# Probabilities of two attentions turned by VectorE and by transfers instead of by TensorE, in three of four rounds each

## Chip, cores and metric

The kernel runs on one core of one Trainium2 chip. The metric is the device time of one execution in microseconds (us), the median of several. A core has five engines with a queue each: TensorE (PE; its weight loads are shown as PEld), VectorE (DVE), ScalarE (ACT), GpSimd (POOL) and SyncE (SP). SP and POOL also issue the transfers (DMA).

## What is computed

Two blocks of a network over 512 tokens of width 1024, in float32. Cut to the parts that the change touches:

```python
# first block: 8 heads of 64, in 4 pairs
q = rms_norm(q, g_q) * 64 ** -0.5; k = rms_norm(k, g_k)
# three dilated causal branches, merged: the kernel computes them as one attention,
# softmax(q k^T + log(number of branches that see the key)) v
y_attn = dilated_mixture(q, k, v)
mix = concat([rms_norm(gb * short_conv(gc * u)), rms_norm(y_attn)])
x = x + mix @ w_out
# second block: 8 heads share one key and one value of 64
p = softmax(where(key in top 128 of the indexer, q k^T * 64 ** -0.5, -inf))
yb = (p @ v) * silu(zb)
```

The modulation of the second block, `silu(c) @ w_mod`, is also summed up during the first attention, on VectorE, from rows that POOL loads.

## The kernel before

**Products.** Almost every product is a `project`: a weight block of 1024 x 128 is loaded (SP, `load`, 512 KB), split into a high part (ACT, `split_hi`) and a low part (DVE, `split_lo`), and multiplied in 24 passes of 512 columns into a PSUM bank (lines 591 to 593). There are two weight buffers for each of raw, high and low part. The high part of block n+2 is made once TensorE has used block n, the low part after it; TensorE waits for `lo_done`. Everything is ordered by semaphores, and each engine works its queue in the order that is written out by hand in its own program.

**First attention, `mix(i, last)`, four rounds, a pair of heads each.** TensorE: three projections (u, gc, gb of the convolution), the transposition of the values into `vtok`, the scores of both heads (`split_scores`: q and k were split into `q1`, `k1`, `k1L` by ACT and DVE, so that two fast passes do for a product), the projections q, k, v of the next pair, then `attend`, then `head_sums` (sums of squares of the next q and k). `attend` does, per head, ten transpositions of 128x128 blocks of the probabilities `L` into four PSUM banks (line 568), which ACT copies out to `pT` (`p_evac`, eight copies), and then the products with the values (line 657). Causality leaves 10 of 16 blocks: a head has 1280 columns of `L`, at `CB`.

DVE in `mix`: `qk_norm`, the low parts of q and k, splits and the convolution, `score_max` (adds the mask, takes the maximum, writes `L`), `mod_rows` (6 rows of the modulation a round, each 128x1024, from `mraw`), `normalise` (times the reciprocal sum, in place). ACT: `head_rsqrt`, the high parts of q and k, `softmax` (exponentials), `p_evac`, and at the round's end the copy and the square of the attended values (`yo`, `sqa`, `mixH`). POOL: `mod_loads`, the six transfers of `mraw` a round, each as soon as its buffer is free.

**Second attention, `att(i, last)`, four rounds.** TensorE: the gate's product (`glu`, 24 passes, the scores of key blocks 2 and 3 in its middle), the projection of the next q, `attend`, and the scores of blocks 0 and 1 of the next pair. Scores here are plain float32 products of 64 rows (`scores`, line 625). DVE: `normalise`, the gate (`sza`), `head_max` with the gating of the attended values (`gate_out`) in its middle. In the last round the projection's place is taken by products of the next stage (`ab_terms`).

```python
def attend(a, v, vcol):
    for hh in range(2):
        pe.wait_ge(pn, a * 2 + (hh + 1))
        for kb in range(TB):
            pe.wait_ge(t_free, a * 8 + (4 * hh + kb + 1))
            transposes(TBANK[kb], [L[:, hh, CB[b] + P * kb:CB[b] + P * kb + P] for b in range(kb, TB)]).then_inc(tr_mm, 1)
    wait(pe, o_free, a + 1)      # the bank of the attended values has been read
    ...                          # products with the values, into OB
```

Of the kernel before, what the change touches and what calls it, by code (L numbers as in the profile page):

```python
# [16 lines left out]
F32 = mybir.dt.float32  # L17
# [59 lines left out]
OFF = [0, 512, 896, 1152, 1280]  # L77

# [49 lines left out]
def program(nc, io):  # L128
# [7 lines left out]
    with ExitStack() as ctx:  # L136
# [34 lines left out]
        mx, nmx, rs, rinv = (at(n, [P, 8]) for n in ("mx", "nmx", "rs", "rinv"))  # L171
# [44 lines left out]
        ybL = at("ybL", [P, KH, S], F32R, B0 + 31744)  # L216
# [13 lines left out]
        q1 = [at(f"q1{e}", [P, S], F32R, B0 + 26624 + 2048 * e) for e in range(2)]  # L230
        k1 = [at(f"k1{e}", [P, S], F32R, B0 + 30720 + 2048 * e) for e in range(2)]
        k1L = [at(f"k1L{e}", [P, S], F32R, B0 + 34816 + 2048 * e) for e in range(2)]
# [41 lines left out]
        q_hi, q_lo, qx_hi, kx_hi = (sem(n) for n in ("q_hi", "q_lo", "qx_hi", "kx_hi"))  # L274
        vtr, vt_done, ych = sem("vtr"), sem("vt_done"), sem("ych")
        sc_ready, sc_free, nm, ex, pn = (sem(n) for n in ("sc_ready", "sc_free", "nm", "ex", "pn"))
# [53 lines left out]
        def freed(eng, s):  # L330

            eng.wait_ge(gfree[s.par], s.gf + 1)

# [90 lines left out]
        def _(pool):  # L424
# [15 lines left out]
            def mod_loads(i):  # L440
# [110 lines left out]

            pool.wait_ge(yb_done, KH)
# [9 lines left out]
        def _(pe):  # L562
# [71 lines left out]
            def split_scores(a):  # L634

                for hh in range(2):
                    for b in range(TB):
                        pe.wait_ge(sc_free, a * 8 + (4 * hh + b + 1))
                        split_score(SB[b], b, q1[hh], k1[hh], k1L[hh]).then_inc(sc_ready, 1)

# [3 lines left out]
            def attend(a, v, vcol):  # L644

                for hh in range(2):
                    pe.wait_ge(pn, a * 2 + (hh + 1))
                    for kb in range(TB):
                        pe.wait_ge(t_free, a * 8 + (4 * hh + kb + 1))
                        transposes(TBANK[kb], [L[:, hh, CB[b] + P * kb:CB[b] + P * kb + P] for b in range(kb, TB)]  # L650
                                   ).then_inc(tr_mm, 1)
                wait(pe, o_free, a + 1)
                for kb in range(TB):
                    pe.wait_ge(t_free, a * 8 + (kb + 9))
                    for hh in range(2):
                        r = slice(HD * hh, HD * hh + HD)
                        ins = mm(OB[r, P * kb:S], v[:, kb, vcol(hh)], pT[:, hh, OFF[kb]:OFF[kb + 1]],  # L657
                                 start=(kb == 0), stop=(kb == TB - 1), skip_group_check=True)
                        if kb == TB - 1:
                            ins.then_inc(pv, 1)  # L660
# [50 lines left out]
            def mix(i, last):  # L711
                for j in range(3):
                    project(Slot(3, j, 6, i))
                freed(pe, Slot(2, 0, 6, i))
                transposes(PB[3], [vT[:, blkc(b)] for b in range(TB)]).then_inc(vtr, 1)
                pe.wait_ge(ss_rd, i * 2 + 2)
                pe.wait_ge(xt_done, KD)
                pe.wait_ge(q_lo, i + 1)
                split_scores(i)
# [52 lines left out]
            with pe.Fori(0, NPAIR - 1) as i:  # L772
                mix(i, False)
            mix(NPAIR - 1, True)
# [198 lines left out]
            scores(NPAIR, qn, kn)  # L973
            project(Slot(N_AT))
            pe.wait_ge(yg_rdy, KH)
            pe.wait_ge(ya_done, KH)

# [92 lines left out]
        def _(act):  # L1070
# [104 lines left out]
            def mix(i, last):  # L1175
# [13 lines left out]
                if not (isinstance(i, int) and i == 0):  # L1189
                    wait(act, ych, i + 1)  # L1190
# [1120 lines left out]
```

## Time and profile before

| | |
|---|---|
| median of 3 runs | 1002.49 us (1002.38 to 1002.98) |
| the profiled execution | 1004.4 us, span 1001.6 us |
| PE busy | 983.9 us, 98% of the span |
| DVE, ACT, POOL busy | 684.2, 439.1, 157.7 us |
| transposition of the probabilities on PE (L568, `L`) | 160 instructions, 20.3 us |
| granted clock | 0.999 |

The span is the time from the first to the last instruction of the profiled execution. A row of the timeline gives the start, the duration, the engine and line, what is written from what, and in brackets the idle time before it and what ended it. PE instructions overlap: each lasts longer than the distance to the next start, so distances of starts are what counts. A float32 product is recorded twice, a transposition once.

### The profile page before, as it was taken

To read this page: it belongs to the slowest core of one execution; us is meant where nothing else is said; L and a number is where in the kernel's file an instruction comes from. 1 tells how busy PE (TensorE), PEld (TensorE's weight loads), DVE (VectorE), ACT (ScalarE), POOL (GpSimd) and SP (SyncE) were. 2 spreads that over 40 slices of the span, in tenths; PEclk is the share of its full clock that TensorE was granted. 3 is DMA by queue.
4 is the path that set the end of the run, shared out by engine and by line. 5 is a ranking of instruction groups with operands and counts; after the bars stand their busy time and mean duration, and the time that the engine had idled before them with its cause. 6 is when DMAs were issued, how large, how long until landed. Compare 5 with 4: busy or idle time off the path is not lost. (4 is left out here: it accounts for less than half of the span.)

```text
span 1001.6 us, 14462 instructions
## 1 busy us (share of the span) xinstructions
PE 983.9 (98%) x4732; PEld 798.4 (80%) x4732; DVE 684.2 (68%) x1221; ACT 439.1 (44%) x729; POOL 157.7 (16%) x274
## 2 busy tenths in 40 slices
PE   6999999999999999999999999999999999999997
PEld 6887787777888888888888877888888887677886
DVE  7787786797667667555426668498978764665656
ACT  5656666644323233233221236945542325563343
POOL 3000100200000000964000001835750000000000
PEclk9999999999999999999999999999999999999999
DMA  7244624352533323244223223322233332123332
GB/s 229 85 144 130 204 76 139 77 155 73 178 100 90 105 85 104 88 143 149 88 102 102 86 75 109 102 85 65 63 105 96 92 105 63 43 64 86 106 93 84
DMA packets 144305, 104.31 MB, mean 104 GB/s; under 512 B 4717, under 2 KB 136045, under 8 KB 144269
## 3 DMA queue, kind: packets, MB, share of 16 engines
q1 hardware_dynamic: 138768, 85.83, 29.1%
q0 software_dynamic: 5264, 17.97, 6.0%
q8 instruction: 19, 0.31, 0.1%
q14 instruction: 18, 0.14, 0.0%
q10 hardware_dynamic: 236, 0.06, 0.0%
HBM read 99.65 MB, written 4.20 MB: 104 GB/s over the span
## 5 line engine op out<-in xcount | busy, mean ns | idle before, releaser
L591 PE MATMUL bank<-hH,wH 128*128 128x512 f32 x840 | 328.7, 391 | 0.1
L593 PE MATMUL bank<-hH,wL 128*128 128x512 f32 x840 | 327.0, 389 | 0.0
L592 PE MATMUL bank<-hL,wH 128*128 128x512 f32 x840 | 326.9, 389 | 0.0
L1506 DVE TENSOR_TENSOR wL<-raw,wH 128x1024 fp32r<-128x1024 f32 x155 | 196.1, 1266 | 129.2 <-ACT wH L1074 128.2
L1074 ACT ACTIVATE wH<-raw 128x1024 fp32r<-128x1024 f32 x155 | 164.2, 1059 | 264.4 <-PE bank L593 136.1
L591 PEld LDWEIGHTS bank<-hH,wH 128*128 128x128 f32 x840 | 157.7, 188 | 36.9 <-issue 2.9
L593 PEld LDWEIGHTS bank<-hH,wL 128*128 128x128 f32 x840 | 157.7, 188 | 32.9
L592 PEld LDWEIGHTS bank<-hL,wH 128*128 128x128 f32 x840 | 157.8, 188 | 32.1
L835 PE MATMUL bank<-aH,wH 128*128 (+1 forms) x160 | 62.2, 389 | 0.0
L836 PE MATMUL bank<-aL,wH 128*128 (+1 forms) x160 | 62.2, 389 | 0.0
L837 PE MATMUL bank<-aH,wL 128*128 (+1 forms) x160 | 62.2, 389 | 0.0
L1817 DVE TENSOR_TENSOR ut<-bank,r 128x512 f32<-128x512 f32 x22 | 15.2, 691 | 50.4 <-PE bank L593 50.4
L443 POOL DMA_DIRECT2D mraw<-in_w_mod_dram x24 | 12.7, 530 | 199.4 <-DVE macc L1685 199.1
L1165 ACT ACTIVATE L<-L,nmx 128x128 f32<-128x128 f32 (+1 forms) x64 | 35.1, 550 | 12.1 <-DVE nmx L1667 11.3
L1685 DVE SCALAR_TENSOR_TENSOR macc<-mraw,csil,macc 128x1024 f32<-128x1024 f32 x24 | 30.3, 1281 | 8.9 <-DMA mraw<-in_w_mod_dram 8.9
L835 PEld LDWEIGHTS bank<-aH,wH 128*128 128x128 f32 x160 | 30.0, 188 | 6.3
L837 PEld LDWEIGHTS bank<-aH,wL 128*128 128x128 f32 x160 | 30.0, 188 | 6.2
L836 PEld LDWEIGHTS bank<-aL,wH 128*128 128x128 f32 x160 | 30.0, 188 | 6.2
L1074 ACT ACTIVATE aH<-a 128x512 f32 (+1 forms) x22 | 13.9, 632 | 45.6 <-DVE a L1821 45.6
L498 POOL COPY yaF<-yg 32x128 f32<-32x128 f32 x64 | 32.8, 512 | 2.9
L1823 DVE TENSOR_TENSOR aL<-a,aH 128x512 fp32r<-128x512 f32 (+1 forms) x22 | 17.0, 771 | 18.3 <-ACT aH L1074 18.3
L553 POOL DMA_DIRECT2D gate_row<-mod x1 | 0.8, 764 | 166.6 <-DVE ybL L2181 166.6
(478 smaller groups left out, 1548.5 us busy)
## 6 DMA issues: line engine op xcount, KB each, us to landing
raw<-in_w_in_dram SPq DMA_DIRECT2D x61, 512.0 KB, 3.6
mraw<-in_w_mod_dram POOLq DMA_DIRECT2D x24, 512.0 KB, 4.6
raw<-in_w_gate_dram SPq DMA_DIRECT2D x22, 512.0 KB, 3.7
raw<-in_w_up_dram SPq DMA_DIRECT2D x22, 512.0 KB, 3.7
raw<-in_w_down_dram SPq DMA_DIRECT2D x22, 512.0 KB, 3.3
raw<-in_w_out_dram SPq DMA_DIRECT2D x16, 512.0 KB, 3.5
x_tok<-in_x_dram SPq DMA_DIRECT2D x4, 512.0 KB, 5.6
rotations<-eb POOLq DMA_DIRECT2D x4, 512.0 KB, 5.0
```

Of the source, the lines that this page charges most:

```text
L498: ins = g.tensor_copy(dst(a, b), src(a, b))
L591: mm(o, a, hH[:, k, :], start=(k == 0), stop=False)
L592: mm(o, a, hL[:, k, :], start=False, stop=False)
L593: ins = mm(o, b, hH[:, k, :], start=False, stop=(k == KD - 1))
L835: mm(PB[d][:], blk(wH[s], d), rh, start=a, stop=False, skip_group_check=True)
L836: mm(PB[d][:], blk(wH[s], d), rl, start=False, stop=False, skip_group_check=True)
L837: ins = mm(PB[d][:], blk(wL[s], d), rh, start=False, stop=False, skip_group_check=True)
L1074: return A(o, i_, ACT.Copy, scale=scale)
L1165: ins = A(l, l, ACT.Exp, bias=nmx[:, c:c + 1], accum_out=rs[:, c:c + 1])
L1506: TT(wL[s.par][:], raw[s.par][:], wH[s.par][:].bitcast(F32), SU).then_inc(lo_done, 1)
L1685: STT(o, mraw[m % 2][:], col(csil, i * 2 + m // 3), o, MU, AD).then_inc(m_used, 1)
L1823: TT(dyn(aL, i), a32[:], dyn(aH, i).bitcast(F32), SU).then_inc(a_done, 1)
```

## The change

In three of four rounds of each attention the probabilities are turned without TensorE and weighed a round later.

- DVE transposes `L` in pieces of 32x32 (`turn`, four instructions a head) into `turned` (second attention: `turned2`). POOL then issues four transfers a round (`turned_moves`), each from 32 partitions of `turned` to all 128 of `pTd`, 1.31 MB in all. They leave the keys of a block in another order (key 32j+c on partition 4c+j), and so the values are put in that order as well: in the copy to `vT`, in the copy of `kvraw` (now two copies), and in products with a permuted identity for the last round of each attention.
- TensorE weighs pair i-1 in round i (`weigh(..., pieces=True)`): in `mix` after the projection of gc, in `att` after the projection of q. `attend` is left for the last rounds, which also weigh the pair before.
- POOL holds the loads of modulation rows 2 to 5 back until the round's moves have landed; DVE does rows 2 to 5 in the next round.
- The scores of the first attention are plain float32 products, as in the second; the split copies of q and k go.
- The negated maximum is taken in one step, and `softmax` runs block by block over both heads.
- In the second attention ACT scales the second head (three rounds), one reciprocal serves both heads, and `gate_out` and `gated_low` come a round later.

```diff
+        turned = at("turned", [P, TB, 2 * NB, 32], F32, B0 + 26624)
+        pTd = at("pTd", [P, TB, 2 * NB, 32], F32, B0 + 10240)
...
+        def places(hh, qb):
+
+            return slice(1 + qb, 1 + qb + 5 * qb + 1, 5) if hh == 0 else slice(5 * qb, 6 * qb + 1)
+
+        def place_of(hh, kb):
+
+            return slice(5 * kb + 1 + kb, 5 * kb + 1 + TB) if hh == 0 else slice(6 * kb, 5 * (TB - 1) + kb + 1, 5)
...
+            def turned_moves(a, src):
+
+                pool.wait_ge(turn_rdy, 2 * TB * (a + 1))
+                settled(pool)
+                for q in range(TB):
+                    pool.dma_start(pTd[:, q].rearrange("p b c -> p (b c)"),
+                                   src[32 * q:32 * q + 32].rearrange("p j b c -> p j (b c)")).then_inc(turn_in, 16)
...
+                    if m == 2 and between is not None:
+                        between()
...
+            def moves_then_wait(i):
+                pool.wait_ge(o_free, i + 1)
+                turned_moves(i, turned)
+                pool.wait_ge(turn_in, 16 * TB * (i + 1))
+                settled(pool)
             with pool.Fori(0, NPAIR - 1) as i:
-                mod_loads(i)
+                mod_loads(i, lambda: moves_then_wait(i))
...
+            for i in range(NPAIR - 1):
+                pool.wait_ge(pv, 2 * (NPAIR + i))
+                turned_moves(NPAIR - 1 + i, turned2)
...
+            def weigh(a, v, vcol, pieces=False):
+
+                wait(pe, o_free, a + 1)
+                for kb in range(TB):
+                    for hh in range(2):
+                        r = slice(HD * hh, HD * hh + HD)
+                        p = (pTd[:, :, place_of(hh, kb), :].rearrange("p i b c -> p b i c") if pieces
+                             else pT[:, hh, OFF[kb]:OFF[kb + 1]])
+                        ins = mm(OB[r, P * kb:S], v[:, kb, vcol(hh)], p,
+                                 start=(kb == 0), stop=(kb == TB - 1), skip_group_check=True)
...
+            def mix(i, first, last):
+                project(Slot(3, 0, 6, i))
+                project(Slot(3, 1, 6, i))
+                if not first:
+                    pe.wait_ge(turn_in, 16 * TB * i)
+                    weigh(i - 1, vtok, pair_cols, True)
+                project(Slot(3, 2, 6, i))
...
+                if last:
+                    for b in range(TB):
+                        for j in range(TB):
+                            ins = mm(PB[3][32 * j:32 * j + 32, blkc(b)], vT[:, P * b + j:P * b + P:TB], ident,
+                                     start=True, stop=True, skip_group_check=True)
+                    ins.then_inc(vtr, 1)
+                else:
+                    transposes(PB[3], [vT[:, blkc(b)] for b in range(TB)]).then_inc(vtr, 1)
...
-                split_scores(i)
+                pe.wait_ge(qn_rdy, i * 2 + 2)
+                scores(i, qn, kn)
...
-                attend(i, vtok, lambda hh: slice(HD * hh, HD * hh + HD))
-                if not last:
+                if last:
+                    attend(i, 0, vtok, pair_cols)
+                else:
                     head_sums(i + 1, Slot(7, 0, 6, i))
...
             scores(NPAIR, qn, kn)
+            for j in range(TB):
+                ins = mm(PB[3][32 * j:32 * j + 32, 0:TB * HD], ident[:, j:P:TB], vt2[:].rearrange("p b n -> p (b n)"),
+                         start=True, stop=True, skip_group_check=True)
...
-                attend(i + NPAIR, vt2, lambda hh: slice(0, HD))
-                if not last:
+                if begun:
+                    pe.wait_ge(turn_in, 16 * TB * (i + (NPAIR - 1)))
+                    weigh(i + (NPAIR - 1), vt2, head_cols, True)
+                if last:
+                    attend(i + NPAIR, 1, vt2n, head_cols)
+                else:
                     freed(pe, Slot(N_AT + 1, 1, 2, i))
                     scores(i + (NPAIR + 1), qn, kn, range(2))
...
-                copy(vT[:], PB[s[2].par][:]).then_inc(gfree[s[2].par], 1)
+                copy(vT[:].rearrange("n (b p j) -> n b p j", b=TB, j=TB),
+                     PB[s[2].par][:].rearrange("n (b j p) -> n b p j", b=TB, j=TB)).then_inc(gfree[s[2].par], 1)
...
+                for u, (hh, b) in enumerate(order):
+                    act.wait_ge(sc_free, a * 8 + (u + 1 + 4))
+                    c = 4 * hh + b
+                    l = L[:, hh, CB[b]:CB[b + 1]]
+                    ins = A(l, l, ACT.Exp, bias=nmx[:, c:c + 1], scale=-1.0, accum_out=rs[:, c:c + 1])
...
-            copy(kvraw[:], PB[0][:]).then_inc(gfree[0], 1)
+            copy(kvraw[0:HD, :], PB[0][0:HD, :])
+            copy(kvraw[HD:P, :].rearrange("n (b p j) -> n b p j", b=TB, j=TB),
+                 PB[0][HD:P, :].rearrange("n (b j p) -> n b p j", b=TB, j=TB)).then_inc(gfree[0], 1)
...
+                if not last:
+                    act.wait_ge(rinv_rdy, i + 1)
+                    for b in range(TB):
+                        l = L[:, 1, CB[b]:CB[b + 1]]
+                        ins = A(l, l, ACT.Copy, scale=rinv[:, 4 + b:5 + b])
+                    ins.then_inc(pn_act, 1)
...
+                if last:
+                    p_evac(1)
                 freed(act, s)
                 copy(dyn(y2H, i), dyn(sza, i), 0.5).then_inc(y2h, 1)
...
+            def turn(hh, qb, to=turned):
+
+                v.transpose(to[:, :, places(hh, qb), :].rearrange("p j b c -> p b j c"),
+                            L[:, hh, CB[qb]:CB[qb + 1]].rearrange("p (b j c) -> p b j c", j=TB, c=32)
+                            ).then_inc(turn_rdy, 1)
...
+                    if turning is not None:
+                        if hh:
+                            turning()
+                        dve.wait_ge(pn, a * 2 + (hh + 1))
+                        for b in range(TB):
+                            turn(hh, b)
...
+                if not first:
+                    mod_rows(i - 1, range(2, 4))
                 split_lo(u.next())
...
+                if not first:
+                    mod_rows(i - 1, range(4, 6))
                 used(gb)
...
-                if not last:
-                    mod_rows(i, range(0, 2))
-                normalise(i)
+                if last:
+                    values_low(i - 1)
+                normalise(i, None if last else lambda: split_lo(Slot(3, 3, 6, i).next()))
...
+                    mod_rows(i, range(0, 2))
...
+                    dve.wait_ge(turn_in, 16 * TB * (i + (NPAIR - 1)))
+                    dve.wait_ge(pn, a * 2 + 1)
+                    for b in range(TB):
+                        turn(0, b, turned2)
+                    dve.wait_ge(pn_act, i + 1)
+                    for b in range(TB):
+                        turn(1, b, turned2)
...
                 if last:
-                    gate_out()
+                    gate_out(i - 1)
+                    gated_low(i - 1)
+                    gate_out(i)
+                    gated_low(i)
```

## Rows read from the trace of the kernel before

**Rows 1.** The page: busy time, share of the span, instructions
```profile
PE 983.9 (98%) x4732; PEld 798.4 (80%) x4732; DVE 684.2 (68%) x1221; ACT 439.1 (44%) x729; POOL 157.7 (16%) x274
```
**Rows 2.** Who TensorE waited for: total us, times, longest
```profile
PE bank L575 <- ACT thg L1414: 0.6, 1, 0.6
```
**Rows 3.** Timeline of PE, first attention, rounds 0 and 1
```profile
54.47 0.30 PE L631 MATMUL bank<-k,q 128*128 128x128 f32 x1
...
57.48 0.40 PE L591 MATMUL bank<-hH,wH 128*128 128x512 f32 x1
...
73.82 1.25 PE L568 MATMUL bank<-cst,L 128*128 128x128 f32 x10
...
76.56 2.37 PE L657 MATMUL bank<-pT,vtok 128*64 128x512 f32 x16
...
79.89 0.50 PE L591 MATMUL bank<-hH,wH 128*128 128x512 f32 x1
80.22 0.40 PE L592 MATMUL bank<-hL,wH 128*128 128x512 f32 x1
```
**Rows 4.** Timeline of PE, second attention, round 0 and its end
```profile
844.47 1.25 PE L568 MATMUL bank<-cst,L 128*128 128x128 f32 x10
...
847.30 2.38 PE L657 MATMUL bank<-pT,vt 128*64 128x512 f32 x16
849.61 0.93 PE L625 MATMUL bank<-kn,qn 64*128 64x128 f32 x8
```
**Rows 5.** Timeline of all engines, eight scores in a row before the second attention
```profile
825.06 3.02 PE L625 MATMUL bank<-kn,qn 64*128 64x128 f32 x16
```
**Rows 6.** Timeline of PE, products with 32 output rows
```profile
603.98 1.96 PE L876 MATMUL bank<-s5W,cTt 128*32 128x128 f32 x64
```
**Rows 7.** Timeline of all engines around the copy of `kvraw`
```profile
621.14 0.60 ACT L1074 ACTIVATE kvraw<-bank 128x512 f32<-128x512 f32 x1 [2.34 <-PE bank L921]
621.79 0.19 PEld L591 LDWEIGHTS bank<-hH,wxH 128*128 128x128 f32 x1 [0.47 <-ACT kvraw L1074]
```
**Rows 8.** Groups by line and form, ACT: busy us, mean ns
```profile
L1074 ACT ACTIVATE s5U<-xaP 32x128 f32<-32x128 f32 x32 | 13.6, 426 | 0.3
```
**Rows 9.** Groups by line and form, DVE
```profile
L1869 DVE STREAM_TRANSPOSE mtr<-macc 128x1024 f32<-128x1024 f32 x3 | 3.7, 1238 | 0.0
```
**Rows 10.** Timeline of DVE, first attention, round 0
```profile
61.42 2.48 DVE L1685 SCALAR_TENSOR_TENSOR macc<-mraw,csil,macc 128x1024 f32<-128x1024 f32 x2
63.81 0.17 DVE L1672 RECIPROCAL rinv<-rs 128x4 f32<-128x4 f32 x1
...
66.61 1.22 DVE L1506 TENSOR_TENSOR wL<-raw,wH 128x1024 fp32r<-128x1024 f32 x1
...
69.77 1.28 DVE L1685 SCALAR_TENSOR_TENSOR macc<-mraw,csil,macc 128x1024 f32<-128x1024 f32 x1 [0.75 <-DMA mraw<-in_w_mod_dram]
```
**Rows 11.** Timeline of POOL, first attention, round 0
```profile
63.34 0.53 POOL L443 DMA_DIRECT2D mraw<-in_w_mod_dram  x1 [47.03 <-DVE macc L1685]
```
**Rows 12.** Line 443, the loads of `mraw` (24 of 512 KB)
```profile
DMA to landing us min/median/max: 3.8/4.6/7.1
```
**Rows 13.** Windows: us, busy of PE, PEld, DVE, ACT, POOL, clock, DMA
```profile
79.89:122.12 42.23, 42.02 (x213) 33.22 (x209) 32.52 (x57) 26.56 (x54) 3.17 (x6) 1.00 0.52 151
849.61:868.50 18.89, 18.68 (x102) 13.35 (x101) 12.17 (x35) 11.41 (x30) 0.00 (x0) 1.00 0.20 57
```
**Rows 14.** Timeline of DVE, second attention, round 1 and the last
```profile
858.01 0.18 DVE L1672 RECIPROCAL rinv<-rs 128x4 f32<-128x4 f32 x1 [0.60 <-ACT L L1165]
...
904.80 0.69 DVE L2169 SCALAR_TENSOR_TENSOR y2L<-sza,y2H 128x512 fp32r<-128x512 f32 x1 [2.91 <-ACT y2H L1074]
```
**Rows 15.** Timeline of ACT, second attention, round 0 and the last
```profile
844.67 0.60 ACT L1074 ACTIVATE qn<-bank 128x512 f32<-128x512 f32 x1 [3.71 <-PE bank L593]
...
901.42 2.83 ACT L1074 ACTIVATE pT<-bank 128x512 f32<-128x512 f32 x8 [1.92 <-PE bank L568]
```
**Rows 16.** Timeline of PE, second attention, last round
```profile
903.57 2.37 PE L657 MATMUL bank<-pT,vt 128*64 128x512 f32 x16
```

More of the change, by code:

```diff
@@ L648, in attend @@
                     for kb in range(TB):
-                        pe.wait_ge(t_free, a * 8 + (4 * hh + kb + 1))
+                        pe.wait_ge(t_free, n * 8 + (4 * hh + kb + 1))
                         transposes(TBANK[kb], [L[:, hh, CB[b] + P * kb:CB[b] + P * kb + P] for b in range(kb, TB)]
                                    ).then_inc(tr_mm, 1)
[L652 to L660, printed above, removed]
+                pe.wait_ge(t_free, n * 8 + 12)
+                weigh(a, v, vcol)
             for s in (ix_ready, xf_tr):
@@ L1169, in p_evac, with values_out @@
+            by_head = [(hh, b) for hh in range(2) for b in range(TB)]
+            in_turn = [(hh, b) for b in range(TB) for hh in range(2)]
+            def p_evac(t):
                 for hh in range(2):
                     for kb in range(TB):
-                        act.wait_ge(tr_mm, a * 8 + (4 * hh + kb + 1))
+                        act.wait_ge(tr_mm, t * 8 + (4 * hh + kb + 1))
                         n = S - P * kb
                         copy(pT[:, hh, OFF[kb]:OFF[kb + 1]], TBANK[kb][:, 0:n]).then_inc(t_free, 1)
-            def mix(i, last):
+            def values_out(a):
+                act.wait_ge(pv, a * 2 + 2)
+                copy(yo[:], OB[:])
+                A(sqa[:], OB[:], ACT.Square)
+                A(dyn(mixH, a + KH), OB[:], ACT.Identity, scale=vec[:, bass.ds(a + V_GATT, 1)]).then_inc(o_free, 1)
@@ L1187, in mix @@
-                key_high(0)
                 used(u)
-                if not (isinstance(i, int) and i == 0):
+                if not first:
                     wait(act, ych, i + 1)
@@ L1427, in att @@
                     split_hi(t.next())
-                act.wait_ge(o_free, i + (NPAIR + 1) + 1)
-                copy(dyn(ybH, i), dyn(szb, i)).then_inc(ybh, 1)
-                if not last:
-                    softmax(i + (NPAIR + 1))
-            with act.Fori(0, NPAIR - 1) as i:
-                att(i, False)
-            att(NPAIR - 1, True)
+                if not first:
+                    act.wait_ge(o_free, i + (NPAIR + 1))
+                    copy(dyn(ybH, i - 1), dyn(szb, i - 1)).then_inc(ybh, 1)
+                if last:
+                    act.wait_ge(o_free, i + (NPAIR + 2))
+                    copy(dyn(ybH, i), dyn(szb, i)).then_inc(ybh, 1)
+                else:
+                    softmax(i + (NPAIR + 1), in_turn)
+            att(0, True, False)
+            with act.Fori(1, NPAIR - 1) as i:
+                att(i, False, False)
+            att(NPAIR - 1, False, True)
             with act.Fori(0, KD // 2) as i:
@@ L1711, in mix @@
                 mark(STT(cv[:], cuP[:, 0:S], col(vec, i + V_CONV), cv[:], MU, AD))
+                if not first:
+                    mod_rows(i - 1, range(4, 6))
                 used(gb)
```

204 lines of the change are left out of this document (94 added, 110 removed).

## The prediction

> **What bounds the kernel now.** I read the page first: TensorE is busy for 983.9 of 1001.6 us [rows 1], so only what leaves its queue, or opens a gap in it, moves the time. The list of what TensorE waited for is short; the one entry that the change touches is 0.6 us for ACT's tanh in the last round of the second attention [rows 2]. Then the timelines of TensorE around `attend`. In the first attention the transpositions of a round begin at 73.82 and the products with the values at 76.56 [rows 3]: 2.74 us, twice the 1.25 of ten transpositions and 0.24 of waiting for `p_evac`. In the second they run from 844.47 to 847.30: 2.83 us [rows 4]. The windows of a round say how much room the helpers have: DVE is busy for 32.5 of 42.2 us in a round of `mix`, for 12.2 of 18.9 us in a round of `att`, and the clock is at its full level (1.00, so 2.4 GHz) in both [rows 13]. So TensorE's share can be read off directly, and the doubt is whether DVE, ACT and the transfers stay hidden in rounds that get shorter.
>
> **What TensorE no longer does.** Twenty transpositions in each of six rounds. Three rounds at 2.74 and one at 2.83 [rows 3, 4]; the other two of `att` I take at 2.75, the same pattern. Together 16.5 us. The products with the values stay, 2.31 us a round (847.30 to 849.61 [rows 4]), only later. They now read `pTd` in runs of 32 columns with jumps between them. No row shows such a read by TensorE; below it is bounded by no extra cost (these products stream at float32's slow pace, so reading is hardly their limit), above by half as much again, 6 × 1.15 = 7 us. I take none.
>
> **Scores of the first attention.** Split, they take 57.48 − 54.47 = 3.01 us a round [rows 3]; as plain products, the same eight before the second attention are busy for 3.02 us with an overlap into what follows [rows 5], about 2.95 by starts. Four rounds: −0.2 us. ACT and DVE lose the split copies, over 4 us of DVE a round, which is what pays for the turning.
>
> **What TensorE gets or waits for.**
> - A change from float32 products to the split passes costs a slower first pass: 0.33 us from 79.89 to 80.22 [rows 3] where 0.23 is usual (16.34 us from 57.48 to 73.82 for 72 passes). Weighing in the middle of the projections adds one such change in three rounds: +0.3.
> - The permuted values of the last round: 16 products of 128 columns with 32 output rows. 64 records of that form (32 products) take 1.96 us [rows 6], so 0.98, for four transpositions of about 0.13 (10 in 1.25 [rows 3]), with their start 0.36: +0.6. The four of 256 columns before the second attention: +0.5 by the same row, 1.0 at most if the four column groups did not overlap.
> - `kvraw`: TensorE already waits for this copy (0.47 [rows 7]), and it becomes two. The first is as before but for half the partitions, the second adds 0.5 at the contiguous pace (0.60 less the overlap), and it reads PSUM at a distance of 32 elements. ACT's copies `s5U<-xaP` read at a distance of four and take 426 ns for 128 columns [rows 8], against some 310 for a contiguous 128 (0.60 for 512 less 384 columns at 0.83 ns, plus a little for SBUF): about twice as long per column. So +0.5 to +1.0; I take +0.8. The Trainium skill (SBUF — State Buffer, Door 1) says that SBUF lines are 16 bytes and PSUM's 8, and that every step to another line costs; the row agrees in direction, and the sum by the page would be the upper end. The same slow read in `vT`'s copy lies behind the v projection, with `p_evac` gone from its place (2.83 [rows 15]): hidden.
> - `att(0)`: `attend` stood between the projection of q and the next scores and hid ACT's copy of `qn` (844.67, 0.60 [rows 15]) out of the bank. In round 0 nothing is weighed, so the scores wait until about 845.4 where the projection ended at 844.47: +0.9. Later rounds have `weigh` there.
> - The last round of `att`. `weigh` of the last pair waits on `o_free`, now for `gate_out` of the pair before, whose place in DVE's queue is behind `y2L`; `y2L` waits for ACT's `y2H`, and that stands behind the eight copies of `p_evac` [rows 15]. In the trace `y2L` starts at 904.80 [rows 14]; `gate_out` behind it, 0.6 later and 0.69 long, ends at 906.1, and with 0.1 of signalling TensorE may weigh at 906.2 instead of 903.57 [rows 16]: +2.6. This is a new wait and the largest cost.
> - The tanh wait goes: the exponentials begin on the first blocks while the last maxima are still being taken, and end some 2 us earlier: −0.6 [rows 2].
>
> **Sum.** −16.5 − 0.2 + 0.3 + 0.6 + 0.5 + 0.8 + 0.9 + 2.6 − 0.6 = −11.6 us. The profiled execution took 1004.4 us with a span of 1001.6; the median of the runs is 1002.49, close to the span. I take the difference off the median: 990.9, say 991.
>
> **Does the rest stay hidden, first attention.** *Turning.* A 32x32 transposition of 128x1024 takes 1.24 us on DVE [rows 9], one column per 1.2 ns with its fixed part. Four of 128 to 512 columns are about 1.7 us a head by that pace (1280 columns and four starts); upper bound for the scattered writes, twice that. *The weights of v.* In the old order normalising begins at 63.81, after 2.48 us of modulation rows, and v's low part is made at 66.61 [rows 10]. Now those rows come later: two normalisations (1.4 each, half of 63.81 to 66.61) and the turning of head 0 (1.9 with its wait) end at about 66.0, the split at 67.2; v begins at 68.4 (57.48 + 10.9). Held, with 1.2 us in hand. *The moves.* Head 1 is turned by about 68.8. POOL then issues four transfers, 1.31 MB. No row shows SBUF to SBUF; the nearest is the pair of `mraw` loads issued from 63.34 on [rows 11], whose second lands at 69.77 [rows 10]: 1.05 MB in 6.4 us, so 8 us here. Bounds from the landing times: 3.8 to 7.1 us for 512 KB [rows 12]; four quarter-megabyte-and-more moves in series at the slow end are 4 × 0.625 × 7.1 = 18 us, at the quick end 6. *Behind them* on POOL stand the loads of modulation [rows 2] and 3. With 8 us the moves end at 76.8, the loads land at 81.4 and 82.6, and DVE, which now has these rows in its queue ahead of gb's split, is done with them at 83.9 and with the split at 85.1. The next round's u begins at 79.89 − 5.05 = 74.85, gb 13.2 later at 88.05. So 2.9 us in hand: moves of up to 11 us cost nothing, and each further microsecond costs one in each of three rounds. The Trainium skill speaks against these moves: by SBUF — State Buffer, Door 1, 32 partitions reach only 8 of the 16 ports, about 218 GB/s at best, and a transfer has some 2 us fixed. An estimate by that page is 1.31 MB / 218 GB/s + 2 = 8 us, no longer than the estimate from rows.
>
> **Second attention.** DVE's 12.2 us a round [rows 13] become 12.2 + 3.6 − 1.2 = 14.6, in a round of 18.9 − 2.75 = 16.1. The chain: exponentials done by about 858 instead of 860, one reciprocal (where 858.01 stands now [rows 14]), head 0 scaled (1.2), both turned (3.6), the gate (0.69 as `y2L` [rows 14]), the split (1.2 [rows 10]), the gate's last step (0.69): free bank at about 865.5. The next gate product starts less than 1 us after 868.50 − 2.75 = 865.75, so about 866.6: held by 1 us. ACT's scaling of head 1 (four copies, about 1.5) runs beside DVE's 2.9 us on head 0. Moves end well ahead of `weigh`.
>
> **Rivals.**
> 1. *DVE becomes the bound.* Were the scattered turning to take twice 1.7 us a head, v's weights would come 0.5 late in three rounds, the moves' margin would be short by 0.5, and `att` would wait about 2.4 us in three rounds: +10, about 1001. For it: both margins are near 1 us. Against: the output still comes in runs of 32, and 1.24 us for 1024 is the plain pace. Smaller versions (+1 to +4) fit between. Together 17%.
> 2. *The moves are slow but not fatal.* 12 to 14 us each: +3 to +10, 994 to 1001. For it: four transfers from 32 partitions each beside weight loads. 12%.
> 3. *Slower than before.* At 18 us, the slow end of [rows 12], gb's weights come 7 us late in three rounds: +21, about 1012. It decides from 15 us on, where 3 × 3.9 eats the gain. 7%.
> 4. *Weighing in pieces is slow*: up to +7, 998. 6%.
> 5. *The turning does not take place off the path at all*, so that no change shows: nothing in the queues speaks for it; 1%.
>
> **Numbers.** My forecast holds with 57%, at 991, with 989.5 to 993 as its own range (the lower end with cheap copies of `kvraw`, the upper with `kvraw` at its bound and half a microsecond a round lost once or twice). The range for 8 in 10: from 989.3 to 998. A measurement of this kernel can tell about 0.2%, 2 us. Faster by more: 57 + nearly all of 1, 2, 4 = 88%; within: 4%; slower: 8%.
>
> **What would show it.** Line 568 with `L` shrinks from 160 to 40 instructions. TensorE's list of waits gets ACT `qn` 0.8, `kvraw` 1.0, and 2.6 before the last `weigh`. The transposes on DVE are at 1.7 to 1.9 us a head. `turn_in` never stops TensorE, and no wait for `wL` appears before gb or v. I am wrong if gb's or v's first pass, or the gate's in `att`, waits for DVE; then look at how long the four moves take, and at the length of one turn of 512 columns (0.7 us expected).

## The result: 5 us faster, under half of the forecast

The changed kernel takes 997.48 us (median of 9 runs, 995.5 to 1000.9), the kernel before 1002.98 us beside it (1002.4 to 1003.6). The ratio is 0.9950, 95% interval 0.9940 to 0.9959: faster by 5.0 us (4.1 to 6.0) where 11.5 were forecast. The time is inside the range, the gain less than half of the one forecast. The runs also lie 5 us apart where those of before lie 1.2 apart. The profiled execution took 999.76 us with a span of 998.2, one of the longer of the nine. One execution of version e9 below took 1643 us at a mean granted clock of 0.56; it is left out of that version's ratio, and why it was slow is not known.

The page's first row, and then, from TensorE's list of waits, those of the changed stages (total us, times, longest; the waits of the kernel's start and one for a row of the input are left out):

```profile
PE 975.0 (98%) x4648; PEld 785.0 (79%) x4648; DVE 679.7 (68%) x1218; ACT 414.3 (42%) x671; POOL 171.2 (17%) x298
```
```profile
PE bank L622 <- DVE wL L1581: 3.1, 2, 2.4
PE bank L676 <- DVE szb L2265: 2.8, 1, 2.8
PE bank L676 <- ACT pT L1132: 0.9, 1, 0.9
PE bank L656 <- DVE nmx L1725: 0.7, 2, 0.6
PE bank L656 <- ACT qn L1132: 0.7, 1, 0.7
PE bank L622 <- ACT kvraw L1132: 0.6, 1, 0.6
```

TensorE is busy 8.9 us less than in [rows 1], but there are more waits than the one of [rows 2], and "busy" includes stretches at a lower clock. Three of the waits were forecast (`szb`, which is `gate_out`, `qn` and `kvraw`). Those for `wL` (gb's low part), `pT` and `nmx` were not.

TensorE's timeline shows where the time goes. These are the starts of rounds 1, 2 and 3, the products with the values in two of them, and the first pass behind `attend`:

```profile
74.93 0.50 PE L622 MATMUL bank<-hH,wH 128*128 128x512 f32 x1
...
86.05 2.38 PE L676 MATMUL bank<-pTd,vtok 128*64 128x512 f32 x16
89.11 0.50 PE L622 MATMUL bank<-hH,wH 128*128 128x512 f32 x1 [0.69 <-DVE wL L1581]
...
116.25 0.50 PE L622 MATMUL bank<-hH,wH 128*128 128x512 f32 x1
...
156.41 0.50 PE L622 MATMUL bank<-hH,wH 128*128 128x512 f32 x1
...
167.53 2.37 PE L676 MATMUL bank<-pTd,vtok 128*64 128x512 f32 x16
172.28 0.47 PE L622 MATMUL bank<-hH,wH 128*128 128x512 f32 x1 [2.38 <-DVE wL L1581]
...
195.82 0.50 PE L789 MATMUL bank<-mixH,wH 128*128 128x512 f32 x1
```

Round 1 starts 4.96 us earlier than in [rows 3] (2.31 of it are products that have only been put off), but round 1 lasts 116.25 − 74.93 = 41.3 us, round 2 40.2, where 39.5 were to be expected (42.23 − 2.74 − 0.06 + 0.11). In round 3 gb waits for 2.4 us. Behind `attend` the changed kernel is at 195.82. The kernel before was there at 195.62:

```profile
190.53 2.66 PE L568 MATMUL bank<-cst,L 128*128 128x128 f32 x20
193.32 2.37 PE L657 MATMUL bank<-pT,vtok 128*64 128x512 f32 x16
195.62 0.50 PE L744 MATMUL bank<-mixH,wH 128*128 128x512 f32 x1
```

In this execution the first attention has gained nothing at all. The second has: its rounds last 879.72 − 863.48 = 16.2 us instead of 18.9 [rows 13].

The wait in round 3 also costs afterwards. The window from the first pass behind it to the last of gb has a mean granted clock of 0.76, so part of it ran at 1.2 instead of 2.4 GHz, and it takes 7.24 us where the same 24 passes take 5.58 in round 2. Columns: length, busy of PE, PEld, DVE, ACT, POOL, clock, DMA:

```profile
172.28:179.52 7.24, 7.24 (x24) 5.54 (x24) 5.98 (x7) 0.00 (x0) 0.00 (x0) 0.76 0.89 281
```

What gb waits for is in the timelines of POOL and of DVE:

```profile
69.00 2.18 POOL L456 DMA_DIRECT2D pTd<-turned  x4 [52.89 <-DVE turned L1730]
81.18 0.54 POOL L464 DMA_DIRECT2D mraw<-in_w_mod_dram  x1 [10.00 <-DMA pTd<-turned]
...
150.47 2.18 POOL L456 DMA_DIRECT2D pTd<-turned  x4 [13.28 <-DVE turned L1730]
162.98 0.54 POOL L464 DMA_DIRECT2D mraw<-in_w_mod_dram  x1 [10.33 <-DMA pTd<-turned]
```
```profile
66.67 1.69 DVE L1730 STREAM_TRANSPOSE turned<-L 128x128 f32<-128x128 f32 x4
...
85.42 2.50 DVE L1756 SCALAR_TENSOR_TENSOR macc<-mraw,csil,macc 128x1024 f32<-128x1024 f32 x2 [6.58 <-DMA mraw<-in_w_mod_dram]
87.83 1.22 DVE L1581 TENSOR_TENSOR wL<-raw,wH 128x1024 fp32r<-128x1024 f32 x1
...
168.50 2.51 DVE L1756 SCALAR_TENSOR_TENSOR macc<-mraw,csil,macc 128x1024 f32<-128x1024 f32 x2 [8.18 <-DMA mraw<-in_w_mod_dram]
```

The turning takes 1.69 us a head, as forecast. From the first move's issue to the first load behind the landed moves it is 12.2 us in round 0 and 12.5 in round 2 (11.2 in round 1); 8 were forecast. VectorE stands idle for 6.6 and 8.2 us before rows 2 and 3, and gb's low part is behind them. The wait in round 3 is 1.7 us longer than the one in round 1, and the moves are only 0.3 of that: from the issue of the first load behind them to VectorE's first step on it there are 4.2 us in round 0 (81.18 to 85.42) and 5.5 in round 2 (162.98 to 168.50).

The forecast wait of 2.6 us in the last round of the second attention, on TensorE and then on DVE:

```profile
893.75 2.72 PE L599 MATMUL bank<-cst,L 128*128 128x128 f32 x20
899.25 3.33 PE L676 MATMUL bank<-pT,vt2n 128*64 128x512 f32 x16 [2.79 <-DVE szb L2265]
902.51 0.79 PE L606 MATMUL bank<-y2H,wH 128*128 128x512 f32 x1
```
```profile
897.81 0.69 DVE L2261 SCALAR_TENSOR_TENSOR y2L<-sza,y2H 128x512 fp32r<-128x512 f32 x1 [6.25 <-ACT y2H L1132]
898.42 0.68 DVE L2265 TENSOR_TENSOR szb<-bank,szb 128x512 f32<-128x512 f32 x1
```

The chain is the one that the prediction describes: `y2H` behind `p_evac`, `y2L` behind it, the gating last. Before, from the first transposition (900.78 by its timeline) to the first pass behind the products (905.87) it was 5.1 us; now it is 8.8. The 3.3 us of the products, instead of 2.37 [rows 16], are again the clock: the mean granted clock is 0.69 from 899.25 to 902.51 and 0.52 up to 904.

### The profile page after: what moved, and what is told of

Its sections match the earlier page's. It is cut to its first block, busy times and chain, and to the rows that moved or that the text cites. A ratio compares the mean times of both kernels' runs of the same rounds, so it can differ in the third digit from the quotient of the medians.

```text
span 998.2 us, 14115 instructions
## 1 busy us (share of the span) xinstructions
PE 975.0 (98%) x4648; PEld 785.0 (79%) x4648; DVE 679.7 (68%) x1218; ACT 414.3 (42%) x671; POOL 171.2 (17%) x298
## 4 chain that ended last, share of the span: by engine, by line
PE 85%; DMA 6%; DVE 5%; issue 2%; ACT 2%; POOL 0%; DVEq 0%; SPq 0%; POOLq 0%
PE bank L622 17%; PE bank L624 16%; PE bank L623 16%; PE bank L882 4%; PE bank L881 4%; PE bank L883 4%; DMA pTd<-turned 3%; PE bank L606 2%; PE bank L607 2%; PE bank L608 2%; DMA mraw<-in_w_mod_dram 2%; PE bank L656 2%; PE bank L789 1%; PE bank L791 1%; PE bank L790 1%
## 5 line engine op out<-in xcount | busy, mean ns | idle before, releaser
L456 POOL DMA_DIRECT2D pTd<-turned x24 | 13.1, 563 | 212.7 <-DVE turned L1730 180.6
L1223 ACT ACTIVATE L<-L,nmx 128x128 f32<-128x128 f32 (+3 forms) x64 | 35.0, 549 | 0.8 <-DVE nmx L1725 0.8
L464 POOL DMA_DIRECT2D mraw<-in_w_mod_dram x24 | 12.8, 532 | 129.5 <-DVE macc L1756 99.2
```

The lines of the kernel that those rows point to most:

```text
L1223: ins = A(l, l, ACT.Exp, bias=nmx[:, c:c + 1], scale=-1.0, accum_out=rs[:, c:c + 1])
```

## The experiments

Times are given as us saved against the kernel before, by the ratio measured beside it (95% interval in brackets; it is 1.3 to 1.7 us to either side). The kernel before took 1003.3 to 1004.3 us. e0 to e3 were measured together, e4 to e7 together, e8 and e9 together, and e10 last, so "more than e0" compares two ratios, and a difference of less than about 2 us is not clear of noise.

**The changed kernel again (e0).**

> The changed kernel as it is, run beside the others, since its own executions lay between 995.5 and 1000.9 us. Theory A (the four moves of a round take 11 to 13 us, and gb's low part stands behind modulation rows that are loaded after them): again a wide spread around 997.5 us, because the time of a move varies from one execution to the next; in the profile TensorE waits before gb for one to five us over the three rounds, and less in the faster executions. Theory B (VectorE's own work is too long, transfers are hidden): a spread as narrow as that of the kernel before, 1 us.

Measured: 995.9 to 1001.4 us with a median of 1000.3, ratio 0.9951 (0.9935 to 0.9967), 4.9 us saved. TensorE waited 1.9 us before gb. The wide spread agrees with theory A but does not show it: e2 below spreads by only 1.9 us although its profile has 2.7 us of waits before gb, e7 by 1.2 with its moves as slow as here, and e6 by 3.5 without such a wait.

**gb's low part ahead of the modulation rows (e1).**

```diff
-                if not first:
-                    mod_rows(i - 1, range(2, 4))
                 split_lo(u.next())
+                if not first:
+                    mod_rows(i - 1, range(2, 4))
```

> On VectorE the low part of gb's weights is made ahead of modulation rows 2 and 3 instead of behind them; nothing else. Theory A: gb's weights no longer depend on the moves. The waits before gb (0.75 and 2.4 us in the profiled execution), the 1.7 us of lower clock behind the second, and part of the waits behind them go: 3 to 6 us faster than the changed kernel, so 992 to 994.5, and the spread narrows to 1 to 2 us. Theory B: VectorE has the same work up to the scores, so the wait only moves from gb to the scores: less than 1.5 us gained.

Measured: 996.59 us, 995.9 to 997.7; ratio 0.9922 (0.9909 to 0.9936), 7.8 us saved, 2.9 more than e0, at the lower edge of what theory A gave. In its profile no wait before gb is left, and the wait for the maxima is 0.2 us, not longer. With the same order the scores do wait longer in two later profiles (1.2 us in e3, 2.6 in e4, 0.2 again in e5), so theory B describes a part that comes and goes: the late rows then hold up the maxima instead of gb.

**The bank of the last round freed early (e2), and both (e3).**

```diff
                 def gate_out(k):
...
+                if last:
+                    gate_out(i - 1)
                 dve.wait_ge(y2h, i + 1)
                 STT(dyn(y2L, i), dyn(sza, i), 0.5, dyn(y2H, i).bitcast(F32), MU, SU).then_inc(y2_done, 1)
...
                 if last:
-                    gate_out(i - 1)
                     gated_low(i - 1)
```

> Last round of the second attention: VectorE gates the values of the pair before ahead of y2L, so that the bank is free before the copies of the last probabilities are done; nothing else. Theory (the bank is held by the order of VectorE's queue): the last products with the values start 2.7 us earlier, and the clock does not fall, which costs about 1 more now: 3 to 4 us faster than the changed kernel, 993.5 to 994.5. Rival (what follows needs the gated values anyway, and these wait for ScalarE): TensorE stops as long, only a little later, and under 1 us is gained.

> Both of the edits above. If both theories hold, the gains add, since the two places are 700 us apart: 6 to 10 us faster than the changed kernel, 988 to 991. If either rival holds, 992 or more.

Measured: e2 994.80 us, 0.9901 (0.9886 to 0.9916), 9.9 us saved, 5.0 more than e0 (3 to 4 expected); the wait for `gate_out` is gone, and the products wait 0.9 us for the copies of the last probabilities instead of 2.8. e3 994.19 us, 0.9896 (0.9881 to 0.9911), only 10.4 saved, where 2.9 + 5.0 on top of e0 would have made 12.8. The gains did not add up, though 2.4 us over four intervals of this width may be noise. The list of waits of e3:

```profile
PE bank L606 <- DVE wL L1581: 1.8, 1, 1.8
PE bank L676 <- ACT pT L1132: 1.7, 2, 0.9
PE bank L656 <- DVE nmx L1725: 1.2, 3, 0.6
```

The first is some 20 us behind the second attention. It is not new: it is 1.3 us in e0, 1.6 in e1 and 1.4 in e2, 0.4 in the kernel before, and absent only in the first profile of the changed kernel. So it takes a share of every version's gain, and it explains at most 0.5 us of the 2.4. The chain of e3 shows for what `wL` is late:

```profile
900.86 12.63 DMA raw<-in_w_a_o_dram
```

A load of 512 KB that takes 12.6 us, where 3 to 4 are usual. `gate_row`, a transfer of 1 KB, was issued by POOL just ahead of it (898.65). The kernel before has the same load at 11.2 us.

**Waiting block by block in the last rounds (e4), the gate's row early (e5).** e4 is e3 and

```diff
-            def weigh(a, v, vcol, pieces=False):
+            def weigh(a, v, vcol, pieces=False, n=None):
...
                 for kb in range(TB):
+                    if n is not None:
+                        pe.wait_ge(t_free, n * 8 + (kb + 9))
...
-                pe.wait_ge(t_free, n * 8 + 12)
-                weigh(a, v, vcol)
+                weigh(a, v, vcol, n=n)
```

e5 is e3 and

```diff
+            pool.dma_start(g_dram.rearrange("a (k p) -> p (a k)", p=P), mod[:, 3 * KD - 2:3 * KD],
+                           allow_slow_non_contiguous=True).then_inc(g_out, 16)
             for i in range(NPAIR - 1):
                 pool.wait_ge(pv, 2 * (NPAIR + i))
                 turned_moves(NPAIR - 1 + i, turned2)
...
             pool.wait_ge(yb_done, KH)
-            pool.dma_start(g_dram.rearrange("a (k p) -> p (a k)", p=P), mod[:, 3 * KD - 2:3 * KD],
-                           allow_slow_non_contiguous=True).then_inc(g_out, 16)
```

> The kernel with both edits (e3_both), and in the last round of each attention TensorE waits for the copies of the probabilities block by block again, as the kernel before did, instead of for all eight before the first product. Theory: this is a term that the prediction left out; 0.77 us in each of two places (transpositions to products: 3.56 us now, 2.79 before) goes, so 1 to 1.5 us less than the kernel with both edits. Rival: what follows is held by the weights of the end anyway (TensorE waited 1.8 us for them there), so only the first attention's half shows: 0 to 0.7 us.

> The kernel with both edits (e3_both), and POOL writes the 1 KB row of the gate, whose elements lie apart, to device memory ahead of the moves of the second attention instead of behind it; nothing else. In that kernel the load of w_a_o issued at 900.9 landed 12.6 us later, beside this transfer, and TensorE waited 1.8 us for its low part. Theory: this transfer holds the load back; without it the load lands in some 4 us, the wait goes, and 1.5 to 2 us are gained. Rival: the two rows that are spread over 128 partitions hold it back; then nothing changes by more than 0.5 us.

Measured: e4 992.74 us, 0.9888 (0.9873 to 0.9903), 11.2 saved; the wait for `pT` (1.7 us in e3) is gone from the list. e5 992.54 us, 0.9891 (0.9876 to 0.9906), 10.9 saved; the wait for `wL` in line 606 is gone. Against e3 both are within the intervals, so their profiles are the evidence, not their times. In that of e5, from 895 to 915 us, the two loads of `w_a_o` land after a median of 3.8 us, with the two rows that the rival blames still issued beside the first:

```profile
raw<-in_w_a_o_dram SPq DMA_DIRECT2D x2, 512.0 KB, 3.8
```

**The loads of rows 2 and 3 right behind the moves (e6).** The changed kernel and

```diff
                 turned_moves(i, turned)
-                pool.wait_ge(turn_in, 16 * TB * (i + 1))
-                settled(pool)
...
                         if hh:
                             turning()
+                        else:
+                            wait(dve, turn_in, a * 16 * TB)
```

> The changed kernel, but POOL issues the loads of modulation rows 2 and 3 right behind the moves and does not wait until these have landed; VectorE waits for the landing before it turns into the same buffer. Theory A (the moves are long because they share the transfer engines): the loads now also run beside the moves, start 10 us earlier and land by 83 to 84 instead of 85.4, so the waits before gb shrink to nothing in most rounds: 2 to 4 us faster than the changed kernel. The moves themselves become a little longer, which costs nothing until TensorE weighs at 86. Rival: loads and moves share so badly that turn_in stops TensorE before it weighs, or the rows come no earlier: no gain.

Measured: 996.22 us, 0.9928 (0.9914 to 0.9942), 7.2 saved, 2.3 more than e0 (the two intervals overlap a little). In its profile no wait is left in the three rounds but 0.2 us for the maxima, and `turn_in` never stops TensorE.

**Who issues the moves (e7).** In the first attention ScalarE issues the four transfers on its own hardware queue:

```diff
+            def moves_by_act(a):
+                act.wait_ge(o_free, a + 1)
+                act.wait_ge(turn_rdy, 2 * TB * (a + 1))
+                settled(act)
+                for q in range(TB):
+                    act.dma_start(pTd[:, q].rearrange("p b c -> p (b c)"),
+                                  turned[32 * q:32 * q + 32].rearrange("p j b c -> p j (b c)")).then_inc(turn1_in, 16)
...
-                    qkv(6, i, i + 1)
+                    qkv(6, i, i + 1, lambda: moves_by_act(i))
```

> The changed kernel, but in the first attention ScalarE issues the four moves on its own hardware queue, behind the copy of the next k (1.5 us later than POOL did), POOL only waits for their landing. Theory A1 (the packets themselves are slow, whoever issues them): from issue to landing 11 to 12 us as before, and since they start later, gb's weights come 1 to 2 us later in each round: 2 to 6 us slower than the changed kernel. Theory A2 (the software queue is what makes them slow): 6 to 8 us to landing, gb's weights in time: 3 to 5 us faster.

Measured: 997.81 us, 0.9940 (0.9926 to 0.9953), 6.0 saved, not distinguishable from e0. ScalarE's queue, then POOL's load behind the landing:

```profile
68.75 0.67 ACTq L1239 DMA_DIRECT2D pTd<-turned  x1
```
```profile
80.91 1.20 POOL L464 DMA_DIRECT2D mraw<-in_w_mod_dram  x2 [64.80 <-DMA pTd<-turned]
```

12.2 us again, 11.3 and 11.5 in the next two rounds: theory A1 for the cause. Two things soften it. ScalarE's queue needed 5.3 us to issue the four (68.75 to 74.04), POOL's 2.2, so equal totals are not equal moves. And its time was missed (2 to 6 us slower than the changed kernel were expected, none came): the queue issued the first move while ScalarE was still copying k, so nothing started later.

**All five edits (e8).**

> All five edits together: gb's low part ahead of the modulation rows, the bank of the last round gated early, products of the last rounds waiting block by block, the gate's row written out early, and the loads of rows 2 and 3 not waiting for the moves. Theory: with the transfers and VectorE's order out of the way, the gain of the transpositions shows: 990 to 991.5 where the kernel before takes 1003.7, that is 1.2 to 1.35% faster. Rival: VectorE's own work in a round is what is short (the scores still wait for the maxima), so it stays at 992 or above.

Measured: 997.22 us, 0.9937 (0.9923 to 0.9950), 6.3 saved: worse than e3, and the scores do wait for the maxima, as the rival has it; the cause is another. The first line of its list of waits, its DVE in round 1, and ScalarE's step in front of it:

```profile
PE bank L654 <- DVE nmx L1724: 5.6, 3, 2.3
```
```profile
79.16 0.75 DVE L1714 SCALAR_TENSOR_TENSOR kn<-kraw,vec,rk 128x512 f32<-128x512 f32 x1 [0.49 <-ACT rk L1214]
86.61 1.23 DVE L1580 TENSOR_TENSOR wL<-raw,wH 128x1024 fp32r<-128x1024 f32 x1 [6.69 <-ACT wH L1131]
87.75 2.48 DVE L1757 SCALAR_TENSOR_TENSOR macc<-mraw,csil,macc 128x1024 f32<-128x1024 f32 x2
```
```profile
85.52 1.06 ACT L1131 ACTIVATE wH<-raw 128x1024 fp32r<-128x1024 f32 x1 [3.04 <-DMA raw<-in_w_in_dram]
```

gb's high part exists only from 86.6. With the split in front VectorE idles until then and does the 2.5 us of the rows afterwards, without waiting for them, when the convolution and the maxima are due (in e6 it took the first row at 83.6). The high part is late because its weights are: their load was issued at 73.8 and landed 11.7 us later, beside the moves and the two loads of rows that e6 puts there. In e1, where these loads come later, it took 8.1 us, and the high part began at 81.5:

```profile
81.52 1.05 ACT L1132 ACTIVATE wH<-raw 128x1024 fp32r<-128x1024 f32 x1
```

Edits e1 and e6 remedy the same wait, and together they bring another one.

**The source of a move (e9).**

```diff
-                                   src[32 * q:32 * q + 32].rearrange("p j b c -> p j (b c)")).then_inc(turn_in, 16)
+                                   (src[32 * q:32 * q + 32].rearrange("p j b c -> p j (b c)") if src is turned2
+                                    else src[:, q].rearrange("p b c -> p (b c)"))).then_inc(turn_in, 16)
```

> The changed kernel, but each of the four moves of the first attention takes its 320 KB from all 128 partitions of the turned tile to the same partitions, instead of from 32 of them (the values then stand in the wrong places; sizes, queue, number and moment of the transfers are the same). Theory P (32 source partitions are what makes a move slow, as the Trainium skill's rule on ports has it): the four land 8 us or less after the first issue instead of 11 to 13, gb's weights are in time, 3 to 5 us faster than the changed kernel. Theory S (moves within SBUF beside 1.2 MB of weight loads are slow whatever partitions they start from): 11 to 13 us again and no change.

Measured: 995.32 us, 0.9917 (0.9902 to 0.9932), 8.3 saved, 3.4 more than e0. No wait before gb is left in its profile. POOL, rounds 0 and 1:

```profile
69.71 2.13 POOL L456 DMA_DIRECT2D pTd<-turned  x4 [53.01 <-DVE turned L1731]
77.33 0.53 POOL L465 DMA_DIRECT2D mraw<-in_w_mod_dram  x1 [5.49 <-DMA pTd<-turned]
...
109.92 2.13 POOL L456 DMA_DIRECT2D pTd<-turned  x4 [15.21 <-DVE turned L1731]
115.82 0.53 POOL L465 DMA_DIRECT2D mraw<-in_w_mod_dram  x1 [3.77 <-DMA pTd<-turned]
```

7.6, 5.9 and (in round 2) 5.9 us instead of 12.2, 11.2 and 12.5, with the same bytes, queue and moment, and beside the same weight loads. Theory S is out, and theory P stands as far as the time goes. The run changes one thing more than the number of source partitions, though: each row now stays on its own partition instead of going to four others. Which of the two makes the move quick is not separated.

**Four edits, without e1 (e10).**

> The five edits together without the first: the modulation rows stand ahead of gb's low part again, as in the changed kernel. With all five the scores waited 2.0, 2.3 and 1.2 us for the maxima, because VectorE stood idle until ScalarE had gb's high part, with the rows already landed behind it. Theory: this order fills that gap as in the kernel with only the loads unwaited, which had no wait before gb and 0.2 us before the scores; the edits of the last rounds and of the gate's row then add their 5 us: 988 to 990 where the kernel before takes 1003.5, 1.35 to 1.55% faster. Rival: the gains overlap, as those of the first two edits did: 991 to 993.

Measured: 990.54 us, 990.2 to 991.3; ratio 0.9873 (0.9857 to 0.9890), 12.7 us saved, the fastest version. It lies between the 988 to 990 of the theory and the 991 to 993 of the rival; 1.27% faster just misses the theory's 1.35%. What is left of waits behind the start and at the changed places:

```profile
PE bank L654 <- ACT qn L1131: 0.7, 1, 0.7
PE bank L620 <- ACT kvraw L1131: 0.6, 1, 0.6
PE bank L654 <- DVE nmx L1724: 0.2, 1, 0.2
```

## Why the forecast was wrong

**The step that failed** is "8 us here" for the moves. The rows it was taken from are loads that write 128 partitions, and nothing in them says what 32 source partitions do. The bounds beside it had a slip as well: four moves in series at 0.625 of the quickest landing of [rows 12] are 4 × 0.625 × 3.8 = 9.5 us, not 6, and at the median of 4.6 they are 11.5. So the text's own formula put 8 us below the quick end. The moves took 11.2 to 12.5 us, beyond the 11 us that the text had worked out as free, and that threshold was about right: with 11.2 us gb did not wait, with 12.2 it came 0.7 us late. This is rival 2, which had been given 12% with "12 to 14 us" as the size. That the measured 997.5 also lies within its 994 to 1001 is partly luck, because half of what was missing comes from other terms. e1, e6 and e9 take the dependence away in three different ways (another order, earlier loads, quicker moves), and save 2.9, 2.3 and 3.4 us more than e0. So this step is worth about 3 us. In the execution profiled first it was more: 3.1 us of waits, and 1.7 us of clock behind the longer one.

**Terms that were mis-sized or missing.**

- *Changes between plain float32 products and passes*: +0.3 in the sum. Round 2 of `mix`, almost free of waits, takes 40.16 us. The forecast's own steps make 42.23 − 2.74 − 0.06 = 39.43, and +0.11. The missing 0.6 is seen piece by piece: the transpositions of the values take 0.53 us to the next start instead of 0.36 (54.41 − 53.88), the 72 passes behind the scores 16.55 instead of 16.34, u and gc 11.12 instead of 11.0, and the scores 0.1 more for a wait of 0.2 for the maxima. gb takes 5.58 instead of 5.45, and that is the +0.11 that was forecast. A change cost 0.1 to 0.2 us in either direction, and in these rounds there is one in front of the scores, one behind them and one in front of the products with the values that the sum does not have. Over four rounds that is some 1.7 us, an estimate from these pieces.
- *Products of the last rounds*: missing. The changed `attend` waits for all eight copies before the first product; before it waited block by block. In the first attention it is 3.56 us from transpositions to products (189.96 to 193.52) instead of 2.79 (190.53 to 193.32), 0.8 us; the wait behind it is gone in e4. In the second it lay inside the longer wait for the bank.
- *The new wait in the last round*: +2.6, right in place, chain and length (2.79). With the clock behind it, it was 8.8 − 5.1 = 3.7 us, and 0.6 more in the next three passes, so 1.7 above the forecast. e2 saves 5.0 (intervals of 1.5 on both sides). The part of the clock is not fixed: behind the same wait of 2.79 us the products took 2.30 us in e6 and e9, at a granted clock of 1.00, and 3.5, 3.7 and 4.5 us in e0, e1 and e7, at 0.65, 0.61 and 0.50.
- *What stands behind*: missing. The end of the kernel has a load that takes 10 to 13 us; arriving there earlier turned it into a wait of 1.3 to 1.8 us in e0 to e3 (0.37 before, none in the first profile of the changed kernel). That is up to 0.9 us for the changed kernel, by e0. e5 shows that issuing the 1 KB row early removes it.

These sum to 3 + 1.7 + 0.8 + 1.7 + 0.9 = 8.1 us at the upper end; 6.5 were missing between 991 and 997.5. The intervals do not allow a closer account. e10 checks it from the other side: by the forecast's terms a kernel without the 2.6 us of the last round would save 14.1 us, and e10 saves 12.7, short by 1.4 with an interval of 1.7, which leaves room for the 1.7 us of the changes and for little else.

**What was right.** The transpositions were worth what they were said to be: a round of the second attention is 2.65 us shorter, and the four edits of e10, which bring none of them back, reach 12.7 us. The turning takes 1.69 us a head (1.7 forecast); `qn` 0.84 (0.9); the permuted values 1.04 and 0.60 us; the tanh wait is gone; the products read the pieces at full pace (2.30 instead of 2.31), so rival 4 is out. Rival 1 is out in its form (slow turning): VectorE is busy for 30.9 us of 40.2 in a round of `mix` and for 13.3 of 16.2 in one of `att`, and the waits for its maxima come to 0.7 us. `kvraw` cost 0.6 instead of 0.8: both copies together take 1.19 us, twice the 0.60 of the one before [rows 7], so the distance of 32 elements cost nothing, and the price taken from [rows 8] did not apply; nor was the cost of each step to another line, which the prediction cites beside it, to be seen.

Open is why the moves last 11.2 us in one round and 12.5 in the next (11.1 to 13.1 in e1, e3 and e4), how much of the 12 us is the weight loads beside them, what makes the executions of the changed kernel spread by 5 us, and why the clock falls behind a wait of 2.8 us in one execution and not in another.

## What to carry over

Price a transfer by a row with the same partitions at both ends, not only the same size. If no such row exists, the range must reach to the point where its cover ends. Before calling a margin, list what stands behind the covered work on every queue, and ask what a delay there does to the clock. Two remedies for one wait can undo each other: after moving a load, look again at the other loads beside it and at the order of the engine that uses them.

## What the runs showed of the hardware

Moving 1.31 MB within SBUF, from the first issue to the next load behind the landing, took 11.2 to 12.5 us from quarters of 32 partitions to all 128 (105 to 117 GB/s) and 5.9 to 7.6 from all 128 to the same 128 (172 to 222 GB/s), both beside weight loads. The Trainium skill (SBUF — State Buffer, Door 1) says that 32 partitions reach only half of the ports and about 218 GB/s; the direction agrees, and the measured rate is half of that figure. That the ports are the reason is not shown here. From POOL's software queue and from ScalarE's the four took the same 12.2 us in all, with the issuing spread over 2.2 and 5.3 us. The windows of the DMA queues say the same per packet. These are the moves in the changed kernel from 69 to 81.2 us, the moves of e9 from 109.9 to 115.8, and the `mraw` loads in the kernel before from 60 to 72:

```profile
q0 software_dynamic: 320, 1.31, 54.9%
```
```profile
q0 software_dynamic: 320, 1.31, 55.6%
```
```profile
q0 software_dynamic: 319, 1.18, 34.3%
```

54.9% of 16 engines over 12.2 us for 320 packets are 0.33 us for one of 4 KB; 55.6% over 5.9 us for the same 320 are 0.16; 34.3% over 12 us for 319 are 0.21.

A transfer of 1 KB whose elements lie apart held back a 512 KB load on another queue: 12.6 us to landing beside it (e3), a median of 3.8 without it (e5). A load of 512 KB also takes longer beside moves and other loads: 8.1 us beside the moves (e1), 11.7 beside the moves and two more loads (e8), 3.6 with neither beside it (e1). ScalarE copied 128x512 out of PSUM at a distance of elements in 0.60 us (`vT`), as fast as in order [rows 15]. In the profiled executions TensorE's clock fell behind waits of 2.3 us (e8), 2.4 (the changed kernel) and, in four profiles of six, 2.8 us; it stayed at its full level behind 2.8 us in e6 and e9, 1.9 in e0 and 1.8 in e3.
